# Gate placement in a PEER router on one core: right rows by Pool alone, left one-hots by DVE in fp32

## The chip, the cores and the metric

The kernel runs on one core of one Trainium2 chip. The metric is device time in microseconds (us) from the start to the end of the one launch. The engines are called PE (matmuls), DVE (vector), ACT (activations and copies), Pool (GpSimd) and SP (which only issues transfers here).

## The reference, cut to what matters

The program is one layer of a streaming encoder on 1152 tokens (9 tiles of 128). Its last part is a PEER layer: each of 8 heads picks 16 of 16384 experts for each token, and an expert's number is a pair of two keys out of 128.

```python
s = jnp.einsum('nhpc,hpkc->nhpk', q, keys.astype(jnp.float32))
sv, si = lax.top_k(s, PEER_TOPK)
comb = sv[:, :, 0, :, None] + sv[:, :, 1, None, :]
cv, ci = lax.top_k(comb.reshape(N, PEER_HEADS, PEER_TOPK * PEER_TOPK), PEER_TOPK)
i1 = jnp.take_along_axis(si[:, :, 0], ci // PEER_TOPK, axis=-1)
i2 = jnp.take_along_axis(si[:, :, 1], ci % PEER_TOPK, axis=-1)
expert = i1 * PEER_NKEYS + i2
gate = jax.nn.softmax(cv, axis=-1)
...
a = jax.nn.gelu(jnp.einsum('nd,nhkd->nhk', hb, ub), approximate=False)
return jnp.einsum('nhk,nhkd->nd', gb * a, vb)
```

## The kernel before, in words

The kernel has four stages one behind the other: modulation, mixing, routing, experts. Routing finds experts and gates. The first 4 tiles keep lists of their picks, and their experts are fetched row by row. The last 5 tiles are handled densely: the expert stage multiplies all 16384 experts with all their tokens, so routing must write a dense array of gates, 128 x 128 for each token, with the 128 gates of the token at the places (first key, second key) and zeros elsewhere. This is the gate placement.

A token's gates are placed by one matmul: the 128 slots lie on the partitions, the left matrix has in row k a one at the first key of slot k, the right one has in row k the gate at the second key. Their product is the token's 128 x 128 array. Tokens go in batches of 8, 16 batches a tile. `left` and `right` have two buffers each (`b % 2`), so batch b may be written when the matmuls of batch b - 2 are done (`wait_for_placed`, L757).

Before the change a batch goes through five steps, each engine in its own written order and with semaphores between:
- DVE (`hot_rows`, L1099) compares the keys of 8 tokens, broadcast, with the counted numbers 0 to 127, first for the right (L1107), then for the left (L1110). Each writes 128 x 1024 one-hots in bf16, tokens innermost.
- Pool (`place`, L834) multiplies the right one-hots by the gates and turns them to fp32 with keys innermost, one operation for 8 tokens (L841).
- ACT (`left_rows`, L898) copies the left one-hots to fp32 with keys innermost (L902).
- PE (`place`, L1187) does 8 tokens' matmuls in two groups of 4 (L1195); each group waits until its half of the bank is free (`placed`).
- ACT (`take_gates`, L905) copies each group out of PSUM (L912), after the left copy of the following batch. SP stores half a tile at a time (L799).

The work around it is written out by hand in `period(choose, done, prepare)`, which each engine has in its own form. In one period DVE makes the lists of tile `choose` (`two_lists`, `best_pairs`, `chosen_ranks`, `softmax`) and calls `rows(b)` for b = 0 to 15 at fixed places between them, so that placement of tile `done` is scattered over the lists. `rows(0)` comes after the first searches of the lists. PE does the query products and scores of tile `prepare`: first the product of block 0, then the turning of the slots of tile `done` (`turn_slots`, L1177), then other products, and then batch after batch with parts of further products (batches 0 to 7) and the scores (9 to 12) between. ACT copies the turned slots to `keyT` and `gateT` (L874, L875), for which DVE and Pool wait (`slotsT`). Tiles 4 to 8 are placed: four periods have lists as well, three of them also a tile to prepare, and in the last there is placement alone.

Pool has nothing else to do in these periods. Ahead of them it counts the numbers (`iota_keys`, L822) and fetches rows for the first tile (L829). SP loads the tokens of the next tile when the query products have used the ones before.

Of the kernel before, what the change touches and what calls it, by code (L numbers as in the profile page):

```python
# [6 lines left out]
BF16 = mybir.dt.bfloat16  # L7
# [5 lines left out]
P = 128  # L13
# [5 lines left out]
PICKED = 4  # L19
# [70 lines left out]
def sbuf(nc, ctx, name, shape, dtype=F32):  # L90
    return ctx.enter_context(nc.sbuf_tensor(name, shape, dtype))
# [605 lines left out]
def routing(nc, ctx, wq, keys, u_table, v_table, ident_in, shared, h2_rows, h2T_tiles, gate_blocks, picks):  # L697
# [2 lines left out]


    S = sems(nc, "route", "passed consts wq experts_in iota h2 keys_ps keysT q_ps q qT_ps qT scores "
                               "scores_used shifted exp gate_ready keyed slotsT_ps slotsT left_hot left "
                               "right_hot right place_ps placed out0 out1 best_key key_wide first_keyed dve expert picked row_in used "
                               "u0 u1 u2 u3 u4 u5 u6 u7")
    HP = HEADS * 2
    WIDE, NARROW = 4, 12
# [2 lines left out]
    with ExitStack() as mem:  # L710
# [20 lines left out]
        rank = sbuf(nc, mem, "rank", [P, 2, HEADS, TOPK], BF16)  # L731
        total = sbuf(nc, mem, "total", [P, HEADS])
        slots = sbuf(nc, mem, "slots", [P, 3, HEADS, TOPK])
        keyT = sbuf(nc, mem, "keyT", [P, 2, P], BF16)
        gateT = sbuf(nc, mem, "gateT", [P, P])
        left_hot = [sbuf(nc, mem, f"left_hot{s}", [P, NKEYS, BATCH], BF16) for s in range(2)]
        left = [sbuf(nc, mem, f"left{s}", [P, BATCH, NKEYS]) for s in range(2)]
        right_hot = [sbuf(nc, mem, f"right_hot{s}", [P, NKEYS, BATCH], BF16) for s in range(2)]
        right = [sbuf(nc, mem, f"right{s}", [P, BATCH, NKEYS]) for s in range(2)]
        dense = [sbuf(nc, mem, f"dense{s}", [P, NKEYS, BLOCK]) for s in range(2)]  # L740
        iota_rank = sbuf(nc, mem, "iota_rank", [P, TOPK, TOPK], BF16)
        iota_keys = sbuf(nc, mem, "iota_keys", [P, NKEYS, BATCH], BF16)
        s_ps = psum(nc, mem, "s_ps", [P, HP, NKEYS])
        q_ps = psum(nc, mem, "q_ps", [P, HALF])
        x_ps = psum(nc, mem, "x_ps", [P, 4, P])
# [72 lines left out]
        @block.gpsimd  # L818
        def _(pool):
            pool.iota(iota_rank[:, :, :], pattern=[[1, TOPK], [0, TOPK]], base=0, channel_multiplier=0,  # L820
                      allow_small_or_imprecise_dtypes=True).then_inc(S.iota, 1)
            pool.iota(iota_keys[:, :, :], pattern=[[1, NKEYS], [0, BATCH]], base=0, channel_multiplier=0,  # L822
                      allow_small_or_imprecise_dtypes=True).then_inc(S.iota, 1)

            def fetch(slot):

                if slot >= 8:
                    pool.wait_ge(S.used, slot - 7)
                pool.indirect_dma_start(  # L829
                    out=fetched[:, slot % 8, :], out_offset=None, in_=u_table,  # L830
                    in_offset=bass.IndirectOffsetOnAxis(ap=ids[:, 0, slot:slot + 1], axis=0))\
                    .then_inc(row_loaded[slot % 8], 16)

            def place(t):  # L834

                d = t - PICKED
                pool.wait_ge(S.slotsT, t * 2 + 2)
                for b in range(BATCHES):
                    wait_for_placed(pool, d, b)
                    pool.wait_ge(S.right_hot, d * BATCHES + b + 1)  # L840
                    nc.gpsimd.tensor_tensor(  # L841
                        right[b % 2][:, :, :], right_hot[b % 2][:, :, :].rearrange("p i t -> p t i"),
                        gateT[:, b * BATCH:(b + 1) * BATCH].rearrange("p (t o) -> p t o", o=1)
                        .to_broadcast([P, BATCH, NKEYS]), ALU.mult).then_inc(S.right, 1)

            def period(choose, done, prepare):
                indexed, placed = split(done)
                if placed is not None:
                    place(placed)
            pool.wait_ge(S.picked, 1)  # L850
            for slot in range(SLOTS):
                fetch(slot)
            periods(pool, period)

        @block.scalar
        def _(act):
# [38 lines left out]
                                     key4[:, :, s, :].rearrange("p h (a o) -> p h a o", o=1)  # L895
                                     .to_broadcast([P, HEADS, TOPK, TOPK]), ACT.Copy).then_inc(S.key_wide, 1)

            def left_rows(d, b):  # L898

                act.wait_ge(S.left_hot, d * BATCHES + b + 1)  # L900
                wait_for_placed(act, d, b)
                nc.scalar.activation(left[b % 2][:, :, :], left_hot[b % 2][:, :, :].rearrange("p i t -> p t i"),  # L902
                                     ACT.Copy).then_inc(S.left, 1)

            def take_gates(d, b):  # L905
                half = b * 2 // BATCHES
                if b * 2 % BATCHES == 0:
# [7 lines left out]
            def period(choose, done, prepare):  # L915
                indexed, placed = split(done)
                if prepare is not None:
                    take_q(prepare, 0)
                if indexed is not None:
                    take_index(indexed)  # L920
                if placed is not None:
                    take_slots(placed)
                if prepare is not None:
                    take_qT(prepare, 0)
                    take_q(prepare, 1)
                for b in range(BATCHES):
                    if placed is not None:
                        left_rows(placed - PICKED, b)
                        if b:
                            take_gates(placed - PICKED, b - 1)  # L930
                    if prepare is not None and b in (4, 8):
                        take_q(prepare, b // 4 + 1)
                    if prepare is not None and b in (1, 5, 9):
                        take_qT(prepare, b // 4 + 1)
                    if choose is not None and b == 6:
                        widen_keys(choose, 0)
                    if choose is not None and b == 12:
                        act.wait_ge(S.shifted, choose + 1)
                        nc.scalar.activation(soft[:, :, :], soft[:, :, :], ACT.Exp).then_inc(S.exp, 1)
                    if choose is not None and b == 14:  # L940
                        widen_keys(choose, 1)
                if placed is not None:
                    take_gates(placed - PICKED, BATCHES - 1)
# [6 lines left out]
        def _(dve):  # L950
# [145 lines left out]
                                        .to_broadcast([P, HEADS, TOPK]), ALU.mult).then_inc(S.gate_ready, 1)  # L1096
                assert own.n == PER_TILE, own.n

            def hot_rows(d, b):  # L1099

                keys_iota = iota_keys[:, :, :]

                def key(n):
                    return keyT[:, n, b * BATCH:(b + 1) * BATCH].rearrange("p (o t) -> p o t", o=1)\
                        .to_broadcast([P, NKEYS, BATCH])
                wait(dve, S.right, d * BATCHES + max(b - 1, 0))
                nc.vector.tensor_tensor(right_hot[b % 2][:, :, :], key(1), keys_iota, ALU.is_equal)\  # L1107
                    .then_inc(S.right_hot, 1)
                wait(dve, S.left, d * BATCHES + max(b - 1, 0))
                nc.vector.tensor_tensor(left_hot[b % 2][:, :, :], key(0), keys_iota, ALU.is_equal)\  # L1110
                    .then_inc(S.left_hot, 1)

            def period(choose, done, prepare):
                indexed, placed = split(done)

                def rows(b):

                    if b == 0 and done is not None:
                        dve.wait_ge(S.slotsT, done * 2 + 2)
                    if placed is not None:  # L1120
                        hot_rows(placed - PICKED, b)
                    if indexed is not None:
                        if indexed == 0 and b == 0:
                            dve.wait_ge(S.row_in, 16)
                        for slot in range(2):
                            use((indexed * BATCHES + b) * 2 + slot)

                if choose is not None:
                    own.loop(choose * PER_TILE)
                    two_lists(choose, rows)  # L1130
                    best_pairs(choose, rows)
                    chosen_ranks(choose, rows)
                    if picks_rows(choose):
                        expert_ids(choose)
                    softmax(choose)
                else:
                    for b in range(BATCHES):
                        rows(b)
# [3 lines left out]
        def _(pe):  # L1142
# [44 lines left out]
            def place(d, b):  # L1187
                n = d * BATCHES + b
                pe.wait_ge(S.left, n + 1)
                pe.wait_ge(S.right, n + 1)  # L1190
                for g in range(2):

                    pe.wait_ge(S.placed, n * 2 + g + 1)
                    for j in range(4):
                        last = nc.tensor.matmul(place_ps[:, g, j, :], right[b % 2][:, g * 4 + j, :],  # L1195
                                                left[b % 2][:, g * 4 + j, :], start=True, stop=True)
                    last.then_inc(S.place_ps, 1)
# [691 lines left out]
```

## Time and profile before

| | us |
|---|---|
| median of 3 runs | 3471.25 (3468.97 to 3473.54) |
| profiled execution, its own time | 3471.15 |
| its span, first to last instruction | 3469.5 |
| PE busy | 3057.1 |
| DVE busy | 2429.8 |
| Pool busy | 1462.9 |
| ACT busy | 935.1 |

The profile is of one execution. Times inside it count from the first instruction. A row of a group has its line, engine, operation, output and inputs, shapes and count; behind the bars stand busy time in us and the mean of one in ns, then the idle time of the engine just ahead of such instructions and what ended it. A row in the order of time has its start, its duration, the instruction and, in brackets, the idle time before it. When instructions of one kind follow each other they are merged into one row with a count. Durations of instructions that follow each other on an engine can overlap a little, so the distance of two starts is a price as well.

### The profile page before, as it was taken

What the parts mean: (1) busy time and instruction counts of PE and PEld (TensorE: products, weight loads), DVE (VectorE), ACT (ScalarE), POOL (GpSimd) and SP (SyncE); (2) the same over time, 40 slices, a digit from 0 to 9 for tenths busy, and PEclk for the clock granted to TensorE, in tenths of its full rate; (3) what the DMA queues carried; (4) which work ended last, traced back from release to release, by engine and by line L of the source; (5) the groups of instructions that cost most, each with busy time, mean ns of one, the idle gap of its engine ahead of it and who ended that gap; (6) DMA issues with size and microseconds to landing.
All of it is one profiled execution on the core that took longest, in us unless ns stands there. A gap on an engine that the chain in (4) does not pass through costs nothing.

```text
span 3469.5 us, 45795 instructions
## 1 busy us (share of the span) xinstructions
PE 3057.1 (88%) x16658; PEld 2341.4 (67%) x16658; DVE 2429.8 (70%) x4977; ACT 935.1 (27%) x1272; POOL 1462.9 (42%) x1188
## 2 busy tenths in 40 slices
PE   8899969544587557999999999999999999999995
PEld 1466634222355455888888888888788888999994
DVE  1233316999988885777777777777777777888888
ACT  0111112111488792122222212222122222222222
POOL 0000001555445565555545555554545554333334
PEclk9999989777799898999999999999999999999998
DMA  9611151666222429999999999998999998677765
GB/s 358 189 61 61 55 189 61 224 228 235 67 104 112 164 116 358 338 325 337 328 332 321 341 340 321 339 326 314 347 333 332 325 338 305 233 233 236 236 231 198
DMA packets 305753, 857.93 MB, mean 247 GB/s; under 512 B 25360, under 2 KB 108816, under 8 KB 303840
## 3 DMA queue, kind: packets, MB, share of 16 engines
q0 software_dynamic: 151344, 551.09, 43.9%
q1 hardware_dynamic: 154189, 305.27, 25.7%
q8 instruction: 52, 0.85, 0.1%
q14 instruction: 60, 0.49, 0.0%
q10 hardware_dynamic: 108, 0.22, 0.0%
HBM read 793.34 MB, written 63.15 MB: 247 GB/s over the span
## 4 chain that ended last, share of the span: by engine, by line
PE 58%; DVE 2%; DMA 1%; POOL 1%; issue 1%; ACT 0%; SPq 0%; DVEq 0%
PE y_ps L1767 25%; PE a_ps L1748 25%; PE picked_ps L1785 5%; PE uT_ps L1735 3%; DMA shared<-in_peer_u,ids 1%; DMA gates<-gate_blocks 1%; DVE quad L1613 0%; POOL shared L1424 0%; POOL quad L1434 0%; DVE shared L1707 0%; DVE shared L1587 0%; DVE shared L1695 0%; DMA quad<-in_peer_v,idsT 0%; DVE quad L1695 0%; DVE quad L1707 0%
## 5 line engine op out<-in xcount | busy, mean ns | idle before, releaser
L1424 POOL DMA_INDIRECT shared<-in_peer_u,ids x384 | 443.9, 1156 | 639.8 <-DVE acts L1600 593.2
L1748 PE MATMUL a_ps<-h_hi,uT_lo 128*128 128x320 f32 x2048 | 643.4, 314 | 1.7 <-DVE h_lo L1683 1.7
L1748 PE MATMUL a_ps<-h_hi,uT_hi 128*128 128x320 f32 x2048 | 633.6, 309 | 0.0
L1748 PE MATMUL a_ps<-h_lo,uT_hi 128*128 128x320 f32 x2048 | 633.5, 309 | 0.0
L1587 DVE TENSOR_TENSOR shared<-shared,y_ps 128x512 f32<-128x512 f32 x640 | 435.7, 685 | 269.7 <-PE y_ps L1767 269.7
L1767 PE MATMUL y_ps<-v_hi,m_lo 128*128 128x512 f32 x1280 | 509.6, 398 | 14.5 <-DVE shared L1587 8.9
L1767 PE MATMUL y_ps<-v_lo,m_hi 128*128 128x512 f32 x1280 | 504.6, 394 | 0.0
L1767 PE MATMUL y_ps<-v_hi,m_hi 128*128 128x512 f32 x1280 | 501.9, 392 | 0.0
L1600 DVE CUSTOM_DVE_ANT_0 shared<-shared 128x1024 f32<-128x1024 f32 x384 | 464.3, 1218 | 21.3 <-DMA shared<-in_peer_u,ids 21.2
L1434 POOL DMA_INDIRECT quad<-in_peer_v,idsT x384 | 407.4, 1061 | 117.7 <-issue 117.7
L1748 PEld LDWEIGHTS a_ps<-h_hi,uT_lo 128*128 128x128 f32 x2048 | 385.7, 188 | 7.1 <-issue 2.1
L1748 PEld LDWEIGHTS a_ps<-h_lo,uT_hi 128*128 128x128 f32 x2048 | 385.8, 188 | 4.9
L1748 PEld LDWEIGHTS a_ps<-h_hi,uT_hi 128*128 128x128 f32 x2048 | 385.3, 188 | 0.0
L1498 ACT ACTIVATE m_all<-a_ps 128x320 f32<-128x320 f32 x256 | 112.0, 437 | 920.1 <-PE a_ps L1748 920.1
L1767 PEld LDWEIGHTS y_ps<-v_hi,m_lo 128*128 128x128 f32 x1280 | 241.7, 189 | 100.1 <-issue 39.4
L841 POOL TENSOR_TENSOR right<-right_hot,gateT 128x1024 f32<-128x1024 bf16 x80 | 217.5, 2720 | 194.8 <-DVE right_hot L1107 121.9
L1489 ACT ACTIVATE uT_hi<-uT_ps 128x512 fp32r<-128x512 f32 x254 | 137.9, 596 | 596.9 <-PE uT_ps L1735 596.9
L1424 POOL DMA_INDIRECT shared<-in_peer_v,ids x128 | 149.6, 1168 | 327.1 <-DVE quad L1613 289.1
L1195 PE MATMUL place_ps<-left,right 128*128 128x128 f32 x1280 | 179.5, 298 | 122.0 <-ACT dense L912 85.4
L1767 PEld LDWEIGHTS y_ps<-v_hi,m_hi 128*128 128x128 f32 x1280 | 241.7, 189 | 53.7
L1767 PEld LDWEIGHTS y_ps<-v_lo,m_hi 128*128 128x128 f32 x1280 | 241.7, 189 | 40.5
L1568 DVE TENSOR_TENSOR m_all<-m_all,gates 128x320 f32<-128x320 f32 x256 | 126.4, 494 | 199.6 <-ACT m_all L1498 189.6
(181 smaller groups left out, 4487.1 us busy)
## 6 DMA issues: line engine op xcount, KB each, us to landing
shared<-in_peer_u SPq DMA_DIRECT2D x128, 512.0 KB, 6.6
v_all<-in_peer_v SPq DMA_DIRECT2D x128, 512.0 KB, 6.2
gate_blocks<-dense SPq DMA_DIRECT2D x10, 4096.0 KB, 11.2
gates<-gate_blocks SPq DMA_DIRECT2D x64, 640.0 KB, 17.4
w_ada<-in_w_ada SPq DMA_DIRECT2D x12, 2048.0 KB, 10.7
x_in<-in_x_prompt SPq DMA_DIRECT2D x16, 512.0 KB, 4.2
shared<-in_w_in SPq DMA_DIRECT2D x8, 768.0 KB, 12.2
shared<-in_peer_wq SPq DMA_DIRECT2D x3, 2048.0 KB, 14.0
```

What stands on the lines that cost most here:

```text
L841: nc.gpsimd.tensor_tensor(right[b % 2][:, :, :], right_hot[b % 2][:, :, :].rearrange("p i t -> p t i"), gateT[:, b * BATCH:(b + 1) * BATCH ...
L1195: last = nc.tensor.matmul(place_ps[:, g, j, :], right[b % 2][:, g * 4 + j, :], left[b % 2][:, g * 4 + j, :], start=True, stop=True)
L1424: pool.indirect_dma_start(out=rows[n % 4], out_offset=None, in_=u_table if n < DOTS else v_table, in_offset=bass.IndirectOffsetOnAxis(ap=i ...
L1434: pool.indirect_dma_start(out=quads[half][q], out_offset=None, in_=v_table, in_offset=bass.IndirectOffsetOnAxis(ap=idsT[:, t, token:token ...
L1489: nc.scalar.activation(uT_hi[s][:, n * 4:n * 4 + 4, :], uT_ps[:, n * 4:n * 4 + 4, :], ACT.Copy)\
L1498: nc.scalar.activation(m_all[j][parity][:, n * GROUP:(n + 1) * GROUP], a_ps[n][:, 0:GROUP], ACT.Gelu).then_inc(S.gelu, 1)
L1568: nc.vector.tensor_tensor(part, part, gates[c % 2][:, n * per:(n + 1) * per, j, :], ALU.mult)\
L1587: nc.vector.tensor_tensor(part, part, y_ps[n % RING][:, :], ALU.add).then_inc(S.y_free, 1)
L1600: nc.vector.tensor_tensor_reduce(out=rows[n % 4], in0=rows[n % 4], in1=token_row, scale=1.0, scalar=0.0, op0=ALU.mult, op1=ALU.add, accum_ ...
L1748: last = nc.tensor.matmul(a_ps[n][:, 0:GROUP], lhs[s][:, k, :], rhs[:, k, tok], start=k == 0 and m == 0, stop=k == KD - 1 and m == 2)
L1767: last = nc.tensor.matmul(y_ps[n % RING][:, :], lhs[j][parity][:, tok], rhs[j][parity][:, col], start=j == 0 and m == 0, stop=j == 1 and m ...
L1785: last = nc.tensor.matmul(picked_ps[n][q * 32:(q + 1) * 32, :], spread[:, half, q, :], quads[half][q][:, n * HALF:(n + 1) * HALF], start=o ...
```

## The change

DVE now makes only the left one-hots, and directly as fp32 with keys innermost, into `left`; it waits there until the batch before last is placed. ACT's copy of them is gone. Pool makes the right rows from the keys and gates: one operation per token compares the counted numbers with the token's key, which is a scalar read per partition, and multiplies by its gate, another such scalar. Every fourth signals, and PE waits for the right rows of each group of 4 by itself. `keyT` is fp32, and the counted numbers are 128 fp32 values instead of 1024 bf16.

```diff
-        keyT = sbuf(nc, mem, "keyT", [P, 2, P], BF16)
+        keyT = sbuf(nc, mem, "keyT", [P, 2, P])
...
-        iota_keys = sbuf(nc, mem, "iota_keys", [P, NKEYS, BATCH], BF16)
+        iota_keys = sbuf(nc, mem, "iota_keys", [P, NKEYS])
...
                     wait_for_placed(pool, d, b)
-                    pool.wait_ge(S.right_hot, d * BATCHES + b + 1)
-                    nc.gpsimd.tensor_tensor(
-                        right[b % 2][:, :, :], right_hot[b % 2][:, :, :].rearrange("p i t -> p t i"),
-                        gateT[:, b * BATCH:(b + 1) * BATCH].rearrange("p (t o) -> p t o", o=1)
-                        .to_broadcast([P, BATCH, NKEYS]), ALU.mult).then_inc(S.right, 1)
+                    pool.sem_inc(S.passed, 1)
+                    for n in range(BATCH):
+                        token = slice(b * BATCH + n, b * BATCH + n + 1)
+                        last = pool.tensor_scalar(right[b % 2][:, n, :], iota_keys[:, :], keyT[:, 1, token],
+                                                  gateT[:, token], ALU.is_equal, ALU.mult)
+                        if n % 4 == 3:
+                            last.then_inc(S.right, 1)
...
-            def left_rows(d, b):
-
-                act.wait_ge(S.left_hot, d * BATCHES + b + 1)
-                wait_for_placed(act, d, b)
-                nc.scalar.activation(left[b % 2][:, :, :], left_hot[b % 2][:, :, :].rearrange("p i t -> p t i"),
-                                     ACT.Copy).then_inc(S.left, 1)
...
-                    if placed is not None:
-                        left_rows(placed - PICKED, b)
-                        if b:
-                            take_gates(placed - PICKED, b - 1)
+                    if placed is not None and b:
+                        take_gates(placed - PICKED, b - 1)
...
-            def hot_rows(d, b):
...
-                wait(dve, S.right, d * BATCHES + max(b - 1, 0))
-                nc.vector.tensor_tensor(right_hot[b % 2][:, :, :], key(1), keys_iota, ALU.is_equal)\
-                    .then_inc(S.right_hot, 1)
-                wait(dve, S.left, d * BATCHES + max(b - 1, 0))
-                nc.vector.tensor_tensor(left_hot[b % 2][:, :, :], key(0), keys_iota, ALU.is_equal)\
-                    .then_inc(S.left_hot, 1)
+            def left_rows(d, b):
+
+                wait_for_placed(dve, d, b)
+                nc.vector.tensor_tensor(
+                    left[b % 2][:, :, :],
+                    keyT[:, 0, b * BATCH:(b + 1) * BATCH].rearrange("p (t o) -> p t o", o=1)
+                    .to_broadcast([P, BATCH, NKEYS]),
+                    iota_keys[:, :].rearrange("p (o i) -> p o i", o=1).to_broadcast([P, BATCH, NKEYS]),
+                    ALU.is_equal).then_inc(S.left, 1)
...
                 pe.wait_ge(S.left, n + 1)
-                pe.wait_ge(S.right, n + 1)
                 for g in range(2):
-
+                    pe.wait_ge(S.right, n * 2 + g + 1)
                     pe.wait_ge(S.placed, n * 2 + g + 1)
```

## Rows read from the trace of the kernel before

**Rows 1.** The page, part 1: busy us, share of the span and instructions of each engine.

```profile
PE 3057.1 (88%) x16658; PEld 2341.4 (67%) x16658; DVE 2429.8 (70%) x4977; ACT 935.1 (27%) x1272; POOL 1462.9 (42%) x1188
```

**Rows 2.** Groups by line and shape in 890 to 1305 us, Pool, PE, ACT, DVE.

```profile
L841 POOL TENSOR_TENSOR right<-right_hot,gateT 128x1024 f32<-128x1024 bf16 x80 | 217.5, 2720 | 194.8 <-DVE right_hot L1107 121.9 <-PE place_ps L1195 72.8
L1195 PE MATMUL place_ps<-left,right 128*128 128x128 f32 x1280 | 179.5, 298 | 122.0 <-ACT dense L912 85.4 <-ACT left L902 24.2 <-POOL right L841 11.9
L902 ACT ACTIVATE left<-left_hot 128x1024 f32<-128x1024 bf16 x80 | 171.1, 2142 | 22.4 <-DVE left_hot L1110 22.4
...
L912 ACT ACTIVATE dense<-place_ps 128x512 f32<-128x512 f32 x160 | 162.4, 1144 | 9.0 <-PE place_ps L1195 8.9
...
L1107 DVE TENSOR_TENSOR right_hot<-keyT,iota_keys 128x1024 bf16<-128x1024 bf16 x80 | 96.4, 1205 | 11.7 <-POOL right L841 9.2 <-ACT gateT L875 2.5
...
L1053 DVE TENSOR_TENSOR work<-rank,iota_rank 128x4096 bf16<-128x4096 bf16 x5 | 11.4, 2279 | 0.0
...
L1064 DVE TENSOR_TENSOR work<-work,key_wide 128x2048 bf16<-128x2048 bf16 x5 | 6.5, 1307 | 8.0 <-ACT key_wide L894 8.0
```

**Rows 3.** Instructions in order of time in the last placed tile: start, us, engine, instruction.

```profile
1246.61 0.68 DVE L1110 TENSOR_TENSOR left_hot<-keyT,iota_keys 128x1024 bf16<-128x1024 bf16 x1
1246.83 2.75 POOL L841 TENSOR_TENSOR right<-right_hot,gateT 128x1024 f32<-128x1024 bf16 x1 [0.69 <-DVE right_hot L1107]
...
1247.21 2.91 DVE L1107 TENSOR_TENSOR right_hot<-keyT,iota_keys 128x1024 bf16<-128x1024 bf16 x1
...
1250.27 2.74 POOL L841 TENSOR_TENSOR right<-right_hot,gateT 128x1024 f32<-128x1024 bf16 x1 [0.69 <-DVE right_hot L1107]
...
1282.34 2.36 POOL L841 TENSOR_TENSOR right<-right_hot,gateT 128x1024 f32<-128x1024 bf16 x1 [1.30 <-PE place_ps L1195]
```

**Rows 4.** In order of time in the second placed tile, PE.

```profile
1012.96 2.08 PE L1195 MATMUL place_ps<-left,right 128*128 128x128 f32 x16
1014.88 1.88 PE L1157 MATMUL q_ps<-shared,h2T 128*128 128x512 f32 x4
1016.71 2.07 PE L1195 MATMUL place_ps<-left,right 128*128 128x128 f32 x16
```

**Rows 5.** In order of time at the turn to the second placed tile.

```profile
979.57 2.41 DVE L1068 TENSOR_TENSOR work<-work 128x2048 bf16<-128x2048 bf16 x3
...
981.04 3.78 PE L1195 MATMUL place_ps<-left,right 128*128 128x128 f32 x16 [3.41 <-ACT dense L912]
...
982.90 0.29 DVE L1094 TENSOR_TENSOR slots<-soft,total 128x128 f32<-128x128 f32 x1
...
984.61 7.93 PE L1157 MATMUL q_ps<-shared,h2T 128*128 128x512 f32 x16
...
993.34 0.28 ACT L875 ACTIVATE gateT<-x_ps 128x128 f32<-128x128 f32 x1
```

**Rows 6.** In order of time at the turn to the last placed tile, and its end.

```profile
1237.49 0.85 PE L1183 MATMUL x_ps<-ident_c,slots 128*128 128x128 f32 x3
...
1238.87 0.27 ACT L875 ACTIVATE gateT<-x_ps 128x128 f32<-128x128 f32 x1
...
1299.71 1.92 ACT L912 ACTIVATE dense<-place_ps 128x512 f32<-128x512 f32 x2 [0.43 <-PE place_ps L1195]
```

**Rows 7.** In order of time just ahead of the first placed tile, DVE.

```profile
892.50 1.22 DVE L1085 CUSTOM_DVE_ANT_0 dense<-dense 128x1024 f32<-128x1024 f32 x1
...
893.64 1.22 DVE L1085 CUSTOM_DVE_ANT_0 dense<-dense 128x1024 f32<-128x1024 f32 x1
```

**Rows 8.** Groups by line and shape over the whole span, Pool: powers and a one-input operation.

```profile
L354 POOL TENSOR_TENSOR vrstd<-vsum,power 128x4 f32<-128x4 f32 x9 | 9.3, 1029 | 77.3 <-DVE vsum L513 77.3
...
L349 POOL TENSOR_TENSOR rstd<-mean,power 128x1 f32<-128x1 f32 x9 | 4.9, 549 | 81.9 <-DVE mean L480 81.9
...
L392 POOL TENSOR_SCALAR_AFFINE_SELECT wmT<-wmT 128x1024 f32<-128x1024 f32 x1 | 1.1, 1097 | 5.2 <-DVE wmT L566 5.2
```

**Rows 9.** The right one-hots over the span: durations in ns, first and last start.

```profile
L1107 DVE TENSOR_TENSOR right_hot<-keyT,iota_keys x80: 665/680/2914, 911.7 to 1288.8; 128x1024 bf16<-128x1024 bf16 x80
```

More of the change, by code:

```diff
@@ L702, in routing @@
     S = sems(nc, "route", "passed consts wq experts_in iota h2 keys_ps keysT q_ps q qT_ps qT scores "
-                               "scores_used shifted exp gate_ready keyed slotsT_ps slotsT left_hot left "
-                               "right_hot right place_ps placed out0 out1 best_key key_wide first_keyed dve expert picked row_in used "
+                               "scores_used shifted exp gate_ready keyed slotsT_ps slotsT left "
+                               "right place_ps placed out0 out1 best_key key_wide first_keyed dve expert picked row_in used "
                                "u0 u1 u2 u3 u4 u5 u6 u7")
@@ L733, in routing @@
         slots = sbuf(nc, mem, "slots", [P, 3, HEADS, TOPK])
-        keyT = sbuf(nc, mem, "keyT", [P, 2, P], BF16)
+        keyT = sbuf(nc, mem, "keyT", [P, 2, P])
         gateT = sbuf(nc, mem, "gateT", [P, P])
-        left_hot = [sbuf(nc, mem, f"left_hot{s}", [P, NKEYS, BATCH], BF16) for s in range(2)]
         left = [sbuf(nc, mem, f"left{s}", [P, BATCH, NKEYS]) for s in range(2)]
-        right_hot = [sbuf(nc, mem, f"right_hot{s}", [P, NKEYS, BATCH], BF16) for s in range(2)]
         right = [sbuf(nc, mem, f"right{s}", [P, BATCH, NKEYS]) for s in range(2)]
@@ L821, in _ @@
                       allow_small_or_imprecise_dtypes=True).then_inc(S.iota, 1)
-            pool.iota(iota_keys[:, :, :], pattern=[[1, NKEYS], [0, BATCH]], base=0, channel_multiplier=0,
+            pool.iota(iota_keys[:, :], pattern=[[1, NKEYS]], base=0, channel_multiplier=0,
                       allow_small_or_imprecise_dtypes=True).then_inc(S.iota, 1)
@@ L1097, in softmax @@
                 assert own.n == PER_TILE, own.n
-            def hot_rows(d, b):
[L1101 to L1105, printed above, removed]
-                wait(dve, S.right, d * BATCHES + max(b - 1, 0))
-                nc.vector.tensor_tensor(right_hot[b % 2][:, :, :], key(1), keys_iota, ALU.is_equal)\
-                    .then_inc(S.right_hot, 1)
-                wait(dve, S.left, d * BATCHES + max(b - 1, 0))
-                nc.vector.tensor_tensor(left_hot[b % 2][:, :, :], key(0), keys_iota, ALU.is_equal)\
-                    .then_inc(S.left_hot, 1)
+            def left_rows(d, b):
[6 more added lines that the diff above has]
+                    ALU.is_equal).then_inc(S.left, 1)
             def period(choose, done, prepare):
@@ L1120, in rows @@
                     if placed is not None:
-                        hot_rows(placed - PICKED, b)
+                        left_rows(placed - PICKED, b)
                     if indexed is not None:
```

## The prediction

> **What bounds the kernel now.** First the page's busy times: PE leads over the whole span, DVE is second, Pool and ACT are busy for less than half of it [rows 1], which says nothing of a single stage. The gates are placed between 890 and 1305 us, so I next read the groups by line and shape in that stretch alone [rows 2], and there the idle time ahead of each. The reader is to see three things. Pool's right rows take 2.72 us in the mean, and Pool is idle for 194.8 us, released by DVE's right one-hots and by the placing matmuls. ACT's left copies take 171.1 us, its gate copies 162.4 us. DVE's right one-hots take 1.21 us in the mean.
>
> That mean is not DVE's own work. In the order of time [rows 3] a one-hot takes 0.68 us alone, but 2.91 us when it starts while Pool's multiply runs, and it ends just behind it; Pool's multiply takes 2.36 us alone and 2.75 us when it starts inside a one-hot. So a DVE operation with two inputs in SBUF and a Pool operation that reads SBUF exclude each other, and one batch costs their sum: the two Pool starts 1246.83 and 1250.27 lie 3.44 us apart, which is 2 x 0.61 and 2.2.
>
> In the middle of a tile three things end together: ACT's copies (2.14 and 2 x 1.14 us a batch, a little overlapped), this sum, and PE, whose placing matmuls and its share of the query products follow each other without a gap (1012.96 to 1016.71, 3.75 us) [rows 2, 4]. So no single engine bounds a batch, and taking work from one is worth only what the next allows.
>
> At the turn of a tile [rows 5] DVE ends the slots at 983.2, PE ends the last placing at 984.8, does a query product of 7.9 us and only then turns the slots; the keys and gates are ready at 993.6. The last two turns have no query product: from the turning at 1237.5 to the gates at 1239.1 it is 1.65 us [rows 6]. The last tile has placement alone and ends with the copy at 1301.6 [rows 6].
>
> **What the change removes, adds and moves.**
>
> ACT loses 80 left copies, 171.1 us [rows 2]. This is worth nothing by itself: ACT then has 2.3 us of gate copies a batch, and Pool (below) and PE have more.
>
> DVE loses 160 one-hots at 0.61 us a start [rows 3] and gets 80 fp32 ones. Operations of 1024 fp32 elements start 1.14 us apart there [rows 7]; I take 1.15, so 1.22 us a batch become 1.15: 6 us in all, hidden behind Pool. The wait on placed matmuls moves from ACT to DVE. Behind it stands the list work of the next tile; who waits for that is the turn of the slots, which also needs PE past the last batch, so while Pool is the slow one it costs nothing extra. Pool no longer waits for the right one-hots. The counting of keys at the start gets shorter and has cover before and after. Queries, stores and the loads on SP's queue are issued as before; a store waits for its gate copies and comes as much later as they do.
>
> **The new term: eight Pool operations a batch, at c each.** No row shows a Pool operation with two scalars read per partition. The nearest rows [rows 8]: a one-input operation on 1024 fp32 elements takes 1.10 us, 1.07 ns an element, so 128 elements are 0.137 us with nothing fixed; a power on one element takes 0.549 us, on four 1.029 us, so 0.16 us an element and 0.39 us fixed for an instruction with two inputs. Between them also stands an eighth of the multiply it replaces, 2.36 / 8 = 0.30 us [rows 3]. Lowest 0.14, highest 0.549 + 0.137 = 0.69. The two sensible prices are 0.30 (cost by elements) and 0.39 + 0.137 = 0.52 (a fixed part for each). I take **c = 0.45 us**: each of the new operations reads three things from SBUF, so a fixed part is the nearer row, though back to back some of it may overlap. Eight are 3.6 us where one of 2.36 us was.
>
> The rows show that fixed part and no cause of it. The Trainium skill, GPSIMD Engine Reference, section Performance pitfalls for Q7 kernels, says that a small read command costs about 102 cycles that do not overlap with the one before. By that estimate c would be 3 x 0.085 + 0.137 = 0.39, and the sum below 3475 us; no run here shows it.
>
> **The sum, along Pool.** It will be Pool that never rests. Each of DVE's left one-hots shuts it out for 1.15 us, 18.4 a tile. The two-input operations of the lists do too: 2.28, two of 1.31, and 2.41 for three halvings [rows 2, 5], 7.3 us a tile while lists are made.
> - First tile: lists come first, the first one-hots start at 911.7 [rows 9]. Pool has made two batches by then, and makes the third when batch 0 is placed: 911.7 + 1.15 + 2.07 [rows 4] = 914.9. Then 14 batches: 112c + 16.1 + 7.3. Then the turn: 1.0 for the second half of the placing, and 984.8 to 993.6, 8.8 [rows 5]. Gates of the second tile: 948.1 + 112c.
> - Second tile: 128c + 18.4 + 7.3 + 9.8 = 128c + 35.5.
> - Third and fourth: the turn is 1.0 + 1.65, so 128c + 28.35 each.
> - Fifth: 128c + 18.4, then half a placing and a copy, 2.0.
>
> The end is at 1060.7 + 624c. With c = 0.45 that is 1341.5 where 1301.6 was [rows 6]: 39.9 us later. The stage behind starts later by that, and nothing in it changes. The profiled execution took 3471.15 us (median of the runs 3471.25, so it stands for them): 3471.1 + 39.9 = **3511 us**. The sum breaks even at c = 0.386. Pool's waits and signals between batches are left out, as are the smaller two-input operations; the gaps in which Pool's own start overlaps a one-hot work the other way.
>
> **The rivals.**
>
> **Cost by elements, c = 0.30: faster.** Then Pool has 2.4 us a batch as now, ACT is out of the way, and DVE waits for one short operation and not for a whole multiply. For it: the multiply costs 2.36 us for 1024 elements with two inputs against 1.10 with one [rows 3, 8], and one input is what the new operation streams. Against it: the power's fixed 0.39 us. The Trainium skill, GPSIMD Engine Reference, section Engine selection, holds one-input work on GpSimd to be roughly at line rate and two-input work not; that rule speaks for the change, and the two rows agree with its direction. Sum: 1060.7 + 187.2 = 1247.9, 53.7 earlier; PE's 3.75 us a batch [rows 4] against Pool's 2.4 + 1.15 gives back 0.18 x 8 x 3 = 4. So 3422 us. It decides below c = 0.386. Chance 0.25.
>
> **A fixed part that overlaps, c near 0.386: no change.** If 0.14 us of the power's 0.39 lies under the operation in front, c is 0.25 + 0.137 and the sum comes out even, 3471 us. The rows of the power stand alone, so they neither forbid nor show it. Chance 0.08 for within 0.2% (7 us, about what a measurement of this kernel can tell from no change; that is 0.011 us of c on each side). The price by read commands, above, lies on this case's edge.
>
> **A full fixed part and more, c over 0.58: much slower.** Pool has not even the overlap of starts; the power of one element alone is 0.549 us [rows 8]. At 0.58 the end is at 1422.6, 121 later, 3592 us; at 0.69 it would be 190 later. Chance 0.10.
>
> **Short Pool operations do not shut out, or are not shut out.** Then 16.1 + 4 x 18.4 + 4 x 7.3 = 119 us fall out of the sum, and with c = 0.45 the time is 3392 us; DVE, with its lists, would take over about there. Against it: [rows 3] show both directions of the exclusion. Chance 0.05.
>
> **How the numbers follow.** Forecast, c from 0.40 to 0.58: 0.52. With the much slower case that makes 0.62 for slower; elements 0.25 and no exclusion 0.05 make 0.30 for faster; 0.08 between. The range goes from 3424 (c = 0.30) to 3594 (c = 0.58); below it lie the case without exclusion and prices under 0.30, above it 0.10. As both signs hold much of the chance: the forecast's own range is 3480 to 3592.
>
> **What would show it.** Right: Pool's group of 640 operations at about 0.45 us from start to start where nothing interferes; Pool's idle time, 194.8 us now, down to the turns of the tiles; a batch every 4.75 us in the last tile, which then takes 78 us; PE idle until Pool's right rows, not until ACT's copies; DVE's left one-hots at 1.2 us and up to 0.5 more. Wrong: Pool operations starting 0.3 us apart, or DVE and Pool operations running inside each other at their undisturbed times.

## The result, and the profile after

The changed kernel takes 3700.11 us (median of 4 runs, 3696.49 to 3701.97) against 3470.11 us: ratio 1.0658, interval 1.0644 to 1.0671. It is 230 us slower; 3511 was forecast, with a range from 3424 to 3594.

The page's busy times come first, as in [rows 1], then the groups by line and shape from 890 to 1560 us, as in [rows 2].

```profile
PE 3176.1 (86%) x16658; PEld 2432.2 (66%) x16658; DVE 2336.7 (63%) x4897; ACT 801.2 (22%) x1192; POOL 1843.4 (50%) x1748
```

```profile
L841 POOL TENSOR_SCALAR right<-iota_keys,keyT,gateT 128x128 f32<-128x128 f32 x640 | 595.7, 945 | 48.0 <-ACT gateT L875 47.7 <-PE place_ps L1181 0.3
L1181 PE MATMUL place_ps<-left,right 128*128 128x128 f32 x1280 | 280.0, 388 | 231.4 <-POOL right L841 150.0 <-DVE left L1093 56.1 <-issue 25.1
...
L905 ACT ACTIVATE dense<-place_ps 128x512 f32<-128x512 f32 x160 | 167.2, 1047 | 382.6 <-PE place_ps L1181 382.5
L1093 DVE TENSOR_TENSOR left<-keyT,iota_keys 128x1024 f32<-128x1024 f32 x80 | 98.7, 1235 | 350.6 <-PE place_ps L1181 334.9 <-ACT gateT L875 15.6
```

Pool's 217.5 us of work became 595.7, and its 194.8 us of idle time 48.0, of which 47.7 are at the starts and turns of the tiles (`gateT`). PE waits for Pool, ACT for PE, and DVE for the placing matmuls: one engine never rests and the others queue behind it.

The same in the order of time, in the last placed tile:

```profile
1443.27 9.77 POOL L841 TENSOR_SCALAR right<-iota_keys,keyT,gateT 128x128 f32<-128x128 f32 x10
...
1443.90 1.23 DVE L1093 TENSOR_TENSOR left<-keyT,iota_keys 128x1024 f32<-128x1024 f32 x1 [5.92 <-PE place_ps L1181]
...
1448.93 2.07 PE L1181 MATMUL place_ps<-left,right 128*128 128x128 f32 x8 [1.00 <-POOL right L841]
1451.05 1.06 ACT L905 ACTIVATE dense<-place_ps 128x512 f32<-128x512 f32 x1 [2.05 <-PE place_ps L1181]
1451.05 1.33 DVE L1093 TENSOR_TENSOR left<-keyT,iota_keys 128x1024 f32<-128x1024 f32 x1 [5.92 <-PE place_ps L1181]
```

From one left one-hot to the next it is 7.15 us a batch. Before, the last tile had 3.44 at its start [rows 3] and 3.67 at its end, from Pool's start at 1282.34 [rows 3] to the next:

```profile
1286.01 2.36 POOL L841 TENSOR_TENSOR right<-right_hot,gateT 128x1024 f32<-128x1024 bf16 x1 [1.31 <-PE place_ps L1195]
```

In the changed kernel DVE does its 1.2 us and waits 5.92 for the next. The last gate copy of the last tile tells where placement ends:

```profile
1529.12 1.02 ACT L905 ACTIVATE dense<-place_ps 128x512 f32<-128x512 f32 x1 [2.04 <-PE place_ps L1181]
```

It ends at 1530.1 us; before, at 1301.6 [rows 6]. That is 228.5 us, nearly the whole loss: from there to the last instruction it is 2170 us, where it was 2168.

The price of one operation without interference stands at the start of the first placed tile, where Pool works ahead of DVE's first left one-hot:

```profile
899.90 4.69 POOL L841 TENSOR_SCALAR right<-iota_keys,keyT,gateT 128x128 f32<-128x128 f32 x6 [16.68 <-ACT gateT L875]
```

Six operations last 4.69 us, the last of them 0.788 (the median of all 640), so the start-to-start price c is (4.69 - 0.788) / 5 = 0.78 us. I had taken 0.45, and 0.69 as the highest.

### The profile page after: what moved, and what is told of

Its sections match the earlier page's. It is cut to its first block, busy times and chain, and to the rows that moved or that the text cites. A ratio compares the mean times of both kernels' runs of the same rounds, so it can differ in the third digit from the quotient of the medians.

```text
span 3700.2 us, 46150 instructions
## 1 busy us (share of the span) xinstructions
PE 3176.1 (86%) x16658; PEld 2432.2 (66%) x16658; DVE 2336.7 (63%) x4897; ACT 801.2 (22%) x1192; POOL 1843.4 (50%) x1748
## 4 chain that ended last, share of the span: by engine, by line
PE 54%; DMA 2%; DVE 1%; issue 1%; POOL 1%; ACT 0%; SPq 0%; DVEq 0%
PE y_ps L1753 23%; PE a_ps L1734 23%; PE picked_ps L1771 5%; PE uT_ps L1721 3%; DMA shared<-in_peer_u,ids 1%; DMA gates<-gate_blocks 0%; DMA shared<-in_peer_v,ids 0%; POOL shared L1410 0%; POOL quad L1420 0%; DVE shared L1693 0%; DMA quad<-in_peer_v,idsT 0%; DVE shared L1573 0%; DVE shared L1681 0%; DVE quad L1599 0%; DVE quad L1681 0%
## 5 line engine op out<-in xcount | busy, mean ns | idle before, releaser
L841 POOL TENSOR_SCALAR right<-iota_keys,keyT,gateT 128x128 f32<-128x128 f32 x640 | 595.7, 945 | 48.0 <-ACT gateT L875 47.7
L1181 PE MATMUL place_ps<-left,right 128*128 128x128 f32 x1280 | 280.0, 388 | 231.4 <-POOL right L841 150.0
L1181 PEld LDWEIGHTS place_ps<-left,right 128*128 128x128 f32 x1280 | 241.9, 282 | 282.9 <-POOL right L841 188.4
L1093 DVE TENSOR_TENSOR left<-keyT,iota_keys 128x1024 f32<-128x1024 f32 x80 | 98.7, 1235 | 350.6 <-PE place_ps L1181 334.9
L827 POOL DMA_INDIRECT dense<-in_peer_u,ids x128 | 172.2, 1346 | 210.9 <-DVE acts L1076 91.3
```

The costliest lines, as they stand in the source:

```text
L827: pool.indirect_dma_start(out=fetched[:, slot % 8, :], out_offset=None, in_=u_table, in_offset=bass.IndirectOffsetOnAxis(ap=ids[:, 0, slot ...
L841: last = pool.tensor_scalar(right[b % 2][:, n, :], iota_keys[:, :], keyT[:, 1, token], gateT[:, token], ALU.is_equal, ALU.mult)
```

## The experiments

Theory: the time is Pool's price c times 624, plus exclusion, and c is what was wrong. The rivals: the scalars read per partition, the stream of elements, or a fixed cost make c; or the loss is partly DVE's new wait, with the lists behind it. The first four runs have one time each, and so has the multiply alone; their effects are far above the 0.2% by which times of one kernel differ.

**Constants for both scalars.**

```diff
-right[b % 2][:, n, :], iota_keys[:, :], keyT[:, 1, token], gateT[:, token], ALU.is_equal, ALU.mult
+right[b % 2][:, n, :], iota_keys[:, :], 5.0, 2.0, ALU.is_equal, ALU.mult
```

> Pool's per-token operations compare with a constant and multiply by a constant, so no scalar is read per partition; the right rows are no longer the gates. The operation of the changed kernel takes 0.788 us alone. If its price is in the two scalars read from SBUF: 0.30 to 0.45 us, and the time 3700 - 624 x (0.788 - c), so 3395 to 3490 us, not below some 3400 where DVE and PE take over. If it is the stream of 128 elements through compare and multiply, or a fixed cost of any Pool instruction of this kind: still 0.75 to 0.79, and 3676 to 3700 us.

It took 3653.0 us, between the two cases that were expected. At the start of the first placed tile:

```profile
900.86 4.22 POOL L841 TENSOR_SCALAR right<-iota_keys 128x128 f32<-128x128 f32 x6 [16.64 <-ACT gateT L875]
```

With 0.642 for one this is (4.22 - 0.642) / 5 = 0.716 us from start to start. The duration had fallen by 0.146, but the starts moved by 0.065 only, and 624 x 0.065 = 41 is nearly the 47 us that the time fell by. So the scalars are not the price: 0.03 us each.

**The key alone, no multiply.**

```diff
-keyT[:, 1, token], gateT[:, token], ALU.is_equal, ALU.mult
+keyT[:, 1, token], None, ALU.is_equal
```

> Pool's operations compare with the key alone and don't multiply by the gate, so the placed gates are ones. If the price is in the scalars, each about 0.2 us: 0.55 to 0.60 us and 3550 to 3580 us. If it is in the number of arithmetic steps per element: 0.55 to 0.65 as well, so this run counts together with the constants: steps would leave that one at 0.79. If it is a fixed cost: 0.79 and 3700 us.

It took 3571.8 us.

```profile
899.81 4.67 POOL L841 TENSOR_SCALAR right<-iota_keys,keyT 128x128 f32<-128x128 f32 x8 [16.66 <-ACT gateT L875]
```

With 0.596 for the last, (4.67 - 0.596) / 7 = 0.582 us: the second step and its scalar cost 0.20. As a scalar costs 0.03, the step itself is 0.165, or 1.3 ns an element.

**Half the columns.**

```diff
-right[b % 2][:, n, :], iota_keys[:, :], ...
+right[b % 2][:, n, 0:64], iota_keys[:, 0:64], ...
```

> Pool's operations write 64 of the 128 columns (the other half of the right rows stays zero). If the price is in the stream: 0.40 to 0.45 us and 3458 to 3490 us. If it is in the scalars or fixed: 64 elements save 0.07 us at 1.07 ns each, 0.72 us and 3657 us.

The other half of the right rows is set to zero once. It took 3561.2 us.

```profile
901.51 3.94 POOL L841 TENSOR_SCALAR right<-iota_keys,keyT,gateT 128x64 f32<-128x64 f32 x7 [16.66 <-ACT gateT L878]
```

(3.94 - 0.572) / 6 = 0.561 us. 64 elements fewer save 0.219, which is 3.4 ns an element where I had 1.07. If the cost is a straight line through these two widths, then of 0.78 us the stream of 128 elements is 0.44, the scalars 0.065, and 0.28 is left for a fixed part. Both cases that were expected missed, which is the finding: stream and fixed part are both large. The Trainium skill, GPSIMD Engine Reference, section Performance pitfalls for Q7 kernels, gives about 102 cycles for a small read command. If each scalar were one, two would be 2 x 0.085 us by that estimate; the run with constants shows 0.065 for both, and the measurement decides.

The time follows c. In the three runs so far it fell by 47, 128 and 139 us, where 624 times the fall of c gives 41, 124 and 137.

**Left one-hots for two batches a tile only.**

```diff
+                if b >= 2:
+                    nc.vector.memset(spare[:, b % 2 * 8:b % 2 * 8 + 8], 0.0).then_inc(S.left, 1)
+                    return
```

> DVE makes the left one-hots of only the first two batches of a tile and writes 8 spare values instead in the other 14, so the other batches are placed with old left ones. If a two-input DVE operation shuts Pool out for its length: a batch in the last tile goes from 7.18 to 8 x 0.788 = 6.3 us, 70 times 0.87 earlier, 3640 us. If the extra time per batch is Pool's own waits and signals: 3700 us.

It took 3635.8 us. Pool's group in the last placed tile, first of the changed kernel, then of this run:

```profile
L841 POOL TENSOR_SCALAR right<-iota_keys,keyT,gateT 128x128 f32<-128x128 f32 x128 | 114.9, 911 | 3.8 <-ACT gateT L875 3.8
```

```profile
L842 POOL TENSOR_SCALAR right<-iota_keys,keyT,gateT 128x128 f32<-128x128 f32 x128 | 101.0, 800 | 3.8 <-ACT gateT L876 3.8
```

The same 128 operations take 13.9 us less when DVE makes no left one-hots beside them. Over the run 70 of these went and 64.3 us: 0.92 us each, a fifth under the 1.15 that the prediction took, and 3636 us where 3640 was expected. Exclusion holds for short Pool operations as for the long one.

**The left part alone** (with the right one-hots and the Pool multiply of the kernel before), and **the right part alone** (with its left one-hots and ACT copy; Pool signals once a batch here, not for each group of 4). Both keep `keyT` in bf16 too and copy the keys a second time as fp32, `keyF`.

```diff
-                nc.vector.tensor_tensor(left_hot[b % 2][:, :, :], key(0), keys_iota, ALU.is_equal)
+                wait_for_placed(dve, d, b)
+                nc.vector.tensor_tensor(left[b % 2][:, :, :], ...keyF..., ...iota_f..., ALU.is_equal)
```

> The left part of the change alone: DVE writes the left one-hots as fp32, ACT copies none; the right one-hots and Pool's one multiply per batch stay as they were. If Pool's operations per token are the whole loss, this is near the kernel before: DVE and Pool exclude each other for 0.61 + 1.15 + 2.2 = 3.96 us a batch against 3.44 (3.67 with ACT's copies in the last tile), 0 to 8 us a tile, 3465 to 3505 us. If DVE's waits for placed matmuls, with the lists behind them, are a part of the loss: over 3540 us.

```diff
-                    nc.gpsimd.tensor_tensor(right[b % 2][:, :, :], ...right_hot..., ...gateT..., ALU.mult)
+                    for n in range(BATCH):
+                        last = pool.tensor_scalar(right[b % 2][:, n, :], iota_f[:, :], keyF[:, 1, token],
+                                                  gateT[:, token], ALU.is_equal, ALU.mult)
```

> The right part alone: Pool's eight operations per batch as in the changed kernel, the left one-hots in bf16 on DVE and ACT's copy as before. If Pool's price decides, nearly the whole loss: 8 x 0.788 + 0.5 to 0.6 of a bf16 one-hot = 6.8 to 6.9 a batch against 7.18, so 3670 to 3685 us. If DVE's waits are a part of the loss: under 3600 us.

Left alone: 3505.13 us, ratio 1.0103 (1.0087 to 1.0120). Right alone: 3665.96 us, ratio 1.0564 (1.0546 to 1.0581). The left part is at the upper edge of what was expected (3505), the right part 4 us under its range; neither is near the 3540 and 3600 that DVE's waits would have needed. Two Pool multiplies of the left part in the last placed tile, and then its groups by line and shape on DVE, from 890 to 1340 us:

```profile
1292.85 3.20 POOL L846 TENSOR_TENSOR right<-right_hot,gateT 128x1024 f32<-128x1024 bf16 x1 [0.69 <-DVE right_hot L1111]
...
1296.75 3.21 POOL L846 TENSOR_TENSOR right<-right_hot,gateT 128x1024 f32<-128x1024 bf16 x1 [0.69 <-DVE right_hot L1111]
```

```profile
L1111 DVE TENSOR_TENSOR right_hot<-keyT,iota_keys 128x1024 bf16<-128x1024 bf16 x80 | 110.9, 1387 | 17.4 <-POOL right L846 15.5 <-ACT gateT L881 1.9
L1114 DVE TENSOR_TENSOR left<-keyF,iota_f 128x1024 f32<-128x1024 f32 x80 | 98.8, 1235 | 6.0 <-PE place_ps L1203 6.0
L1057 DVE TENSOR_TENSOR work<-rank,iota_rank 128x4096 bf16<-128x4096 bf16 x5 | 20.0, 4001 | 0.0
...
L1030 DVE TENSOR_TENSOR soft<-pair 128x128 f32<-128x128 f32 x4 | 9.8, 2458 | 0.0
```

A batch costs 3.90 us, near the sum 0.61 + 1.15 + 2.2 = 3.96 of exclusion. DVE waits only 6.0 us for placed matmuls, so its new wait is not the loss. What suffers is the list work: the operation that took 2.28 us before [rows 2] takes 4.00 in the mean, and four short groups of 0.28 to 0.41 us take 0.95 to 2.61, as they now often start while Pool's multiply runs. These five groups last 37 us longer together. The first of the short groups, in the kernel before and then in the changed kernel:

```profile
L1026 DVE TENSOR_TENSOR soft<-pair 128x128 f32<-128x128 f32 x4 | 1.1, 279 | 0.0
```

```profile
L1017 DVE TENSOR_TENSOR soft<-pair 128x128 f32<-128x128 f32 x4 | 1.1, 284 | 0.0
```

So in the changed kernel, with Pool's short operations, this loss is not there. The right part alone shows what the left part costs in its place, Pool's time:

```profile
L848 POOL TENSOR_SCALAR right<-iota_f,keyF,gateT 128x128 f32<-128x128 f32 x640 | 547.5, 873 | 57.8 <-ACT gateT L882 54.8 <-PE place_ps L1199 2.9
```

With fp32 left one-hots instead of bf16 ones beside them the same operations take 595.7. So it is luck that the two losses, 35 and 196 us, add up to 231 where together they were 230. With ACT's copies gone and Pool's multiply kept, nothing was gained in sum.

**The multiply alone, no compare.**

```diff
-keyT[:, 1, token], gateT[:, token], ALU.is_equal, ALU.mult
+gateT[:, token], None, ALU.mult
```

> Pool's operations multiply the counted numbers by the gate and compare with nothing, so the right rows are not one-hots. With compare alone the operation took 0.596 us and the time was 3572 us; of the full 0.788 us the stream of 128 elements is 0.43 (from the run with 64), the two scalars 0.146. If the compare is what makes the stream slow, 128 elements cost the 0.137 us of the one-input row before: 0.21 + 0.07 + 0.14 = 0.42 us and some 3460 to 3480 us. If any arithmetic step costs the same: 0.60 us and 3570 us.

It took 3574.7 us, 125 less, where 624 times the fall of c gives 124.

```profile
902.89 5.25 POOL L841 TENSOR_SCALAR right<-iota_keys,gateT 128x128 f32<-128x128 f32 x9 [16.67 <-ACT gateT L875]
```

With 0.598 for the last, (5.25 - 0.598) / 8 = 0.582 us, the same as with the compare. It is not the compare that is slow; each arithmetic step costs.

**The same operations on DVE.** In the first run DVE makes left and right, in the second the right rows and bf16 left one-hots that ACT copies; Pool makes nothing in either.

```diff
-                nc.vector.tensor_tensor(right_hot[b % 2][:, :, :], key(1), keys_iota, ALU.is_equal)
+                for n in range(BATCH):
+                    last = nc.vector.tensor_scalar(right[b % 2][:, n, :], iota_f[:, :], keyF[:, 1, token],
+                                                   gateT[:, token], ALU.is_equal, ALU.mult)
```

> Pool makes nothing: DVE makes the left one-hots as fp32 and the right rows with the same eight operations per batch that the changed kernel gives to Pool; ACT copies none. No exclusion is left. An operation on 128 elements took DVE 0.21 us, about 0.16 from start to start, so a batch costs DVE 8 x 0.16 + 1.15 = 2.45 us. In the last tile a batch then takes 2.5 us against 3.67, 18 us earlier; in the four tiles with lists DVE has 16 x (2.45 - 1.22) = 20 us more work and loses some 17 us of exclusion and 6 of waits, so about as before. 3445 to 3470 us. If DVE's operation costs 0.25 and more, over 3500 us.

> Pool makes nothing: DVE makes the right rows with eight operations per batch and the left one-hots in bf16, which ACT copies as before. DVE has 0.61 + 1.3 = 1.9 us a batch without exclusion, against 1.22 with some 1.1 of it. The last tile stays at ACT's 3.67 us a batch; the four tiles with lists get up to 10 us shorter each, unless ACT and PE, at 3.73 us a batch, hold them: 3430 to 3470 us.

3496.17 us, ratio 1.0077 (1.0060 to 1.0093), and 3477.16 us, ratio 1.0021 (1.0011 to 1.0030). Both missed their ranges; the first comes near the 3500 that went with a price of 0.25 us and more. The first run's order of time in the last placed tile:

```profile
1285.35 1.22 DVE L1114 TENSOR_TENSOR left<-keyF,iota_f 128x1024 f32<-128x1024 f32 x1
1286.48 2.14 DVE L1111 TENSOR_SCALAR right<-iota_f,keyF,gateT 128x128 f32<-128x128 f32 x8
...
1288.54 1.22 DVE L1114 TENSOR_TENSOR left<-keyF,iota_f 128x1024 f32<-128x1024 f32 x1
```

Eight operations take 2.06 us from start to start (1286.48 to 1288.54), 0.257 each and not 0.16. That is a third of Pool's price for the same thing, but in the tiles with lists DVE has no room for it: it was busy for 359 of their 370 us, where it was for 300 of 338 before. 0.1 us more an operation than expected is 12 us a tile, enough for the second run's miss too. In the last tile, with no lists, a batch takes 3.19 us against 3.67. So that tile alone was given to DVE:

```diff
                     if placed is not None and choose is None:
                         both_rows(placed - PICKED, b)
                     elif placed is not None:
                         hot_rows(placed - PICKED, b)
```

> The kernel before, but in the last placed tile, which has no lists beside it, DVE alone makes left and right as in the run where it made both, and Pool and ACT copy nothing. There a batch took 3.19 us where the kernel before takes 3.67: 16 x 0.48 = 7.7 us earlier, 3462 us against 3470, ratio 0.998. The four tiles with lists are untouched. If DVE's pace in that run came from something else than the end of exclusion and of ACT's copies, no gain.

```profile
1271.30 1.24 DVE L1127 TENSOR_TENSOR left<-keyF,iota_f 128x1024 f32<-128x1024 f32 x1
1272.44 2.15 DVE L1124 TENSOR_SCALAR right<-iota_f,keyF,gateT 128x128 f32<-128x128 f32 x8
...
1274.48 1.24 DVE L1127 TENSOR_TENSOR left<-keyF,iota_f 128x1024 f32<-128x1024 f32 x1
```

3.18 us a batch again, and 3461.62 us, ratio 0.9976 (0.9966 to 0.9986): 8.7 us earlier than the kernel before, where 7.7 were expected. This version beats both, if only by 0.24%.

## Why the prediction was wrong, point by point

**The bound: right.** Pool never rests outside the turns, each left one-hot shuts it out, and everything else waits for it. The direction was right.

**The term c: the step that failed.** The prediction bounded the new operation by its nearest rows, "Lowest 0.14, highest 0.549 + 0.137 = 0.69", and took 0.45. It is 0.78, above the highest, and 3700 us lies beyond the range for that. The fixed part was well read: 0.39 from the power, 0.28 + 0.065 as the runs show it. The stream was not: it stood in the 0.45 with 0.137 us and is 0.44. Its 1.07 ns an element came from one row of an operation of another kind [rows 8], and this kind takes 3.4 ns with two arithmetic steps, 1.3 of them for the second. Why an element takes Pool that long, no run shows. A row of the same engine is no bound if the arithmetic differs. The multiply's 2.36 / 1024 = 2.3 ns [rows 3] with one step stood beside it and would have given a warning: with that rate and the fixed part, 0.39 + 0.30 = 0.69 is not a far end but a start.

**The sum, with c measured.** 624 x (0.78 - 0.45) = 206 on top of the 39.9 forecast. The prediction's 1.15 us for each of 78 left one-hots were 0.92, which is 18 less. The turns took longer: from Pool's last operation to the gates it is 10.9 to 12.0 us and not 9.8 where a product lies between, and about 1 more at the other two and at the end, some 6 together. The first tile began 1.8 earlier. 39.9 + 206 - 18 + 6 - 2 = 232, where 228.5 was measured; these parts are read off after the fact, and the rest stays open.

**DVE and ACT.** That DVE's wait costs nothing behind a slow Pool was right: at three of the tiles' starts DVE itself waited for the gates, 15.6 us in all, so its lists were not late. That ACT's 171.1 us are worth nothing behind a slow Pool fits too, as ACT waited 382.5 us for PE. The left part by itself made the kernel slower by 35 us, which the prediction had not asked.

**The rivals.** Cost by elements alone took an eighth of the multiply, 2.3 ns an element and nothing fixed. One step is indeed near that, 3.4 - 1.3 = 2.1 ns; the second step and the 0.345 us beside the stream were missing. The Trainium skill, GPSIMD Engine Reference, section Engine selection, holds one-input work to be roughly at line rate; this one-input work does not agree, with 3.4 ns an element against the 1.07 of the one-input row [rows 8]. Exclusion that spares short operations fell with the run of two left one-hots. The much slower case came true, but its c was placed at 0.58 to 0.69 and its chance at 0.10, and not for its reason: it wanted a larger fixed part, and it was the stream that was larger. Two slips changed nothing: 3.75 less 2.4 + 1.15 is 0.20 and not 0.18, and the ends of the range lie 2 us above the 3422 and 3592 of their cases.

## What to carry to other kernels

When a change gives an engine an operation that the trace does not show, the price needs a rate per element of the same arithmetic, and a count of steps; take the slowest rate on that engine as one end, not the fastest, and add to it for a second step. Splitting one operation of 1024 elements into eight of 128 pays the fixed part eight times. Where two engines shut each other out, add their times per batch before asking which one is freed.

## What the runs showed of the hardware that was not expected

Pool's operation with two scalars and two steps costs 3.4 ns for each element between 64 and 128, by that rate about 0.28 us fixed, and some 0.03 us for each scalar read per partition. With one step a compare and a multiply cost the same, 0.582 us. The same operation of 128 elements costs DVE 0.257 us. A DVE operation of 0.28 us lasts 2.46 when it starts while Pool's multiply of 1024 elements runs. A Pool operation's duration is not its pace: with constants it lasts 0.642 us and starts every 0.716.

PE's granted clock was lower in the changed kernel's placing. The windows of the last placed tile, before and after, with PE's busy time and granted clock:

```profile
1238.00:1302.00 64.00, 34.14 (x258) 31.22 (x256) 50.37 (x32) 60.51 (x51) 41.18 (x16) 0.97 0.31 132
```

```profile
1412.00:1530.00 118.00, 65.96 (x256) 57.00 (x256) 19.84 (x16) 33.14 (x32) 114.94 (x128) 0.50 0.17 71
```

The columns are the window, its length, busy time and count of PE, weight loads, DVE, ACT and Pool, then clock, share of the DMA engines and GB/s. The granted clock was 0.97 before and 0.50 after, which is the lower level of 1.2 GHz. It fell to that ahead of this tile:

```profile
1130.00:1260.00 130.00, 90.40 (x362) 63.40 (x363) 58.08 (x232) 41.14 (x44) 118.78 (x129) 0.76 0.24 97
1260.00:1390.00 130.00, 68.26 (x272) 59.01 (x272) 64.58 (x236) 38.34 (x38) 126.20 (x131) 0.53 0.15 65
```

Up to 1262 PE still had query products and scores between the placings. Behind that it placed four tokens and waited 1 us or more for Pool's right rows, over and over. Four tokens' matmuls then take 2.07 us, which is what eight took before [rows 4]. PE is not the bound, so this costs only the longer turns, about 1 us each, and 2 at the first, where the query product too ran in part at the lower clock.
